# Where VectorE runs the second stream of a modulation unit inside a slot of the seven-product scheme

## What is computed

```python
mod_l = (jax.nn.silu(c) @ w_ada[l] + b_ada[l]).reshape(b_, 1, N_MOD, D_MODEL)
mod_c = (jax.nn.silu(c_ctx) @ w_ada[l] + b_ada[l]).reshape(N_MOD, D_MODEL)
...
def swiglu(h, w_in_ff, w_out_ff):
    gu = h @ w_in_ff
    g, u = gu[..., :D_FF], gu[..., D_FF:]
    return (jax.nn.silu(g) * u) @ w_out_ff
```

## Time and profile before

| | us |
|---|---|
| median of 3 runs (2509.43 to 2518.34) | 2512.81 |
| the profiled execution's own time | 2510.58 |
| its span, first to last instruction | 2508.8 |
| TensorE busy in it | 2441.8 (97%) |
| VectorE busy in it | 1760.4 (70%) |

### The profile page before, as it was taken

The page is one execution under the profiler, slowest core; times in us unless marked ns, Lnnn a source line. Parts: engine busy times, 40 slices in busy tenths (PEclk is TensorE's granted clock), DMA queues, the critical chain, the costliest instruction groups (busy, mean ns, idle before and its releaser), DMA issues.

```text
span 2508.8 us, 33516 instructions
## 1 busy us (share of the span) xinstructions
PE 2441.8 (97%) x12904; PEld 2189.9 (87%) x12904; DVE 1760.4 (70%) x2226; ACT 1068.2 (43%) x1497; POOL 486.2 (19%) x355
## 2 busy tenths in 40 slices
PE   7999999999999999999999999999999999999998
PEld 4999998888987899999888999998888777888787
DVE  5799997676576879888766799786655687522233
ACT  5344433444453743444354544443444555412222
POOL 0344440000500034543000244550000500000000
PEclk9999999999999999999999999999999999999999
DMA  6233336542111243333644433337433203422221
GB/s 256 110 126 131 145 126 252 184 158 83 52 33 66 101 160 134 117 116 128 247 159 148 168 110 126 133 142 256 173 131 108 84 18 135 168 100 97 87 101 67
DMA packets 100364, 328.29 MB, mean 131 GB/s; under 512 B 7809, under 2 KB 38049, under 8 KB 86945
## 3 DMA queue, kind: packets, MB, share of 16 engines
q1 hardware_dynamic: 83040, 316.33, 35.1%
q10 hardware_dynamic: 17218, 10.55, 1.4%
HBM read 318.28 MB, written 8.57 MB: 130 GB/s over the span
## 4 chain that ended last, share of the span: by engine, by line
PE 78%; DVE 13%; issue 5%; DMA 2%; ACT 2%; ACTq 0%; SPq 0%; DVEq 0%
PE ps L2217 29%; PE ps L2177 19%; PE ps L2165 17%; PE ps L931 5%; DVE junk L1772 3%; DVE w_all L2022 2%; DMA acc<-w_ada_t 1%; DVE w_all L1752 1%; PE ps L2259 1%; DVE arena L672 1%; PE ps L1000 1%; PE ps L1071 1%; PE ps L1058 1%; PE ps L955 1%; PE ps L2269 1%
## 5 line engine op out<-in xcount | busy, mean ns | idle before, releaser
L2217 PE MATMUL ps<-w_all,hj_all 128*128 128x512 f32 x2856 | 656.3, 391 | 6.4 <-DVE arena L831 2.5
L2217 PEld LDWEIGHTS ps<-w_all,hj_all 128*128 128x128 f32 x2856 | 535.1, 188 | 119.9 <-issue 3.7
L1752 DVE TENSOR_TENSOR w_all<-raw,w_all 128x2048 fp32r<-128x2048 f32 x156 | 360.5, 2311 | 294.2 <-ACT w_all L1390 294.1
L2177 PE MATMUL ps<-xn_hi,w_all 128*128 128x384 f32 x1728 | 454.1, 336 | 11.7 <-DVE gate_row L2073 11.1
L2165 PE MATMUL ps<-xn_hi,w_all 128*128 128x384 f32 (+2 forms) x1600 | 423.5, 348 | 8.9 <-DVE xn_lo L1830 7.6
L1390 ACT ACTIVATE w_all<-raw 128x2048 fp32r<-128x2048 f32 x157 | 296.9, 1891 | 242.4 <-PE ps L2217 204.6
L1772 DVE SCALAR_TENSOR_TENSOR junk<-acc,silu_row 128x1024 bf16<-128x1024 f32 x224 | 329.8, 1472 | 15.8 <-issue 6.0
L2177 PEld LDWEIGHTS ps<-xn_hi,w_all 128*128 128x128 f32 x1728 | 313.2, 188 | 19.1 <-DVE gate_row L2073 19.0
L2165 PEld LDWEIGHTS ps<-xn_hi,w_all 128*128 128x128 f32 x1600 | 288.8, 189 | 32.3 <-DVE xn_lo L1830 7.8
L2177 PE MATMUL ps<-xn_lo,w_all 128*128 128x384 f32 x864 | 288.7, 334 | 0.0
L2165 PE MATMUL ps<-xn_lo,w_all 128*128 128x384 f32 (+2 forms) x800 | 277.7, 347 | 0.0
(11 more groups left out here) (236 smaller groups left out, 3077.4 us busy)
## 6 DMA issues: line engine op xcount, KB each, us to landing
raw<-w_ff_in SPq DMA_DIRECT2D x104, 1024.0 KB, 4.8
raw<-w_ff_out SPq DMA_DIRECT2D x77, 1024.0 KB, 5.0
acc<-w_ada_t SPq DMA_DIRECT2D x128, 512.0 KB, 3.3
raw<-w_out SPq DMA_DIRECT2D x16, 1024.0 KB, 4.9
raw<-w_in SPq DMA_DIRECT2D x12, 1024.0 KB, 5.7
x<-x_in SPq DMA_DIRECT2D x12, 512.0 KB, 10.8
gate_row<-gate_out_rows ACTq DMA_DIRECT2D x12, 512.0 KB, 7.4
x_out<-x SPq DMA_DIRECT2D x12, 512.0 KB, 9.0
```

Of the source, the lines that this page charges most:

```text
L1752: nc.vector.tensor_tensor(w_lo[par][:, 0:width], raw[par][:, 0:width], w_hi[par][:, 0:width].bitcast(F32), ALU.subtract).then_inc(S["w_lo" ...
L2177: ins = mm(ps[:, bank_, 0:GW], w[:, c], x_[:, k, :], start=start and k == 0 and a == 0, stop=k == 3 and a == 2, skip_group_check=True)
L2217: ins = mm(ps[:, 2 * i + hf, :], xx[:, i * P:(i + 1) * P], w[:, c, hf * 512:(hf + 1) * 512], start=first and c == 0 and a == 0, stop=last ...
```

## The change

The unit is written as two calls of a new function, one for each stream. In a fast slot the first unit's first stream stays where it was, and its second stream now stands behind sum B and low part 1 (in a stage's last slot: behind sum B and the weights of the output product). A slot's second unit, and the units elsewhere, keep both streams together. A unit with one stream has nothing behind sum B. No other engine's instructions change.

```diff
+            def unit_stream(count, half, u, s):
+                n_streams = streams(half)
+                if s >= n_streams:
+                    return
+                if s == 0:
+                    if u == 0:
+                        dve.wait_ge(S["fin_read"], half)
+                    dve.wait_ge(S["ada_raw"], count * 16 + 16)
+                dve.wait_ge(S["ada_used"], count * 2 + (s + START))
+                ins = nc.vector.scalar_tensor_tensor(out=junk[:], in0=acc[:].rearrange("p a n -> p (a n)"), scalar=1.0,
+                                                     in1=silu_row[:, s, :], op0=ALU.mult, op1=ALU.mult,
+                                                     accum_out=ada_col[:, u, s:s + 1])
+                ins.then_inc(S["ada_used"], 2 // n_streams)
+                if u == 3 and s == n_streams - 1:
+                    finish_units(half, half % HALVES, count + 1)
+
             def unit(count, half, u):
...
+                for s in range(2):
+                    unit_stream(count, half, u, s)
...
-                    unit(*units[0])
+                    unit_stream(*units[0], 0)
                     dve.wait_ge(S["snap"], tq * 3 + 3)
                     dve.wait_ge(S["prod"], tq * 6 + 5)
                     nc.vector.tensor_tensor(p5, p5, ps[:, a, 0:GW], ALU.add).then_inc(S["c22"], 1)
...
                     else:
                         split_w(n + 1, par0)
+                    unit_stream(*units[0], 1)
                     dve.wait_ge(S["prod"], tq * 6 + 6)
                     nc.vector.tensor_tensor(u_h, u_h, ps[:, b, 0:GW], ALU.add).then_inc(S["c12"], 1)
```

More of the change, by code:

```diff
@@ L1760, in hj @@
                 nc.vector.tensor_tensor(lo[:, 0:w], hidden(sub, g, c), hi[:, 0:w].bitcast(F32), ALU.subtract).then_inc(S["hj_lo"], 1)
-            def unit(count, half, u):
[L1764 to L1777, removed]
+            def unit_stream(count, half, u, s):
[13 more added lines that the diff above has]
+                    finish_units(half, half % HALVES, count + 1)
+            def unit(count, half, u):
+                for s in range(2):
+                    unit_stream(count, half, u, s)
             def add_bias(h, hl, src):
```

## The result

The changed kernel takes 2520.28 us (median of 14 runs, 2515.19 to 2527.48), the kernel before 2510.39 us (14 runs beside them): a ratio of 1.0038, 95% interval 1.0028 to 1.0047, about 10 us slower. The profiled execution took 2524.53 us, 4.2 above its own median; that of before stood on its median. So the two traces differ by 14.0 us, somewhat more than the kernels do. The length of stage 1 also varies from one execution to the next: two later runs whose program is that of the kernel before up to the last slot of stage 1 have it at 270.2 and 270.9 us, where the trace of before has 272.4. A stage's length can be read to some 2 us there, and to a few tenths in stages 2 and 3.

The account below looks back on a forecast made before the run. The kernel was taken as bound by TensorE, with 17.3 us lost to waits. Terms 11 + 4.6 + 1.0 − 0.6 = 16 on the profiled 2510.6 give 2526.6, about 2528 as median; range 2508 to 2540 us.

Parts of the forecast that it names:

- the gain term: Fast stages: without stream 1 ahead, sum B is ready 2.1 us earlier; at most 17.3 us can be had.
- the loss term: Two-unit slots: the second unit's 3.6 us load is no longer covered; VectorE idles 1.9 us in place of 0.4.
- Stage 1, +11: Stage 1 slot by slot: four groups give 12.4 us, less 1.4 for the earlier sum B at the start.
- two-unit interval: Stage 1, from slot 5's sum B to slot 6's: 15.4 us becomes 16.7, set by VectorE.
- The four groups: Stage 1, groups of four slots (2, 2, 2, 1 units): each 63.0 us where it is 59.9, +3.1.
- The check on stage 1: VectorE's busy time there, less 5 us for GpSimd's hold, plus 27 idle: 277 us, more than the present 272.4.
- End of stage 1, +4.6: Stage 1's last slot: late hidden tile and SyncE's queue behind stream 1 delay the output product by 4.6 us.
- upper bound of 6.0: End of stage 1: the delay if SyncE's queue moves as one piece, 6.0 us; the lower bound was 1.2.
- Stages 2 and 3, +1.0 and −0.6: Stages 2 and 3: 1.2 us back each, 0.2 lost per later two-unit slot, 1.2 at stage 2's end.
- GpSimd's hold, 0.3 us less a slot: VectorE, per slot: stream 1 gains 1.0 us and low part 1 loses 0.7; bounds 0 to 1.0.
- it works as written: Rival: sum B comes early and the 17.3 us come back wholly or in part, about 2500 us; chance 0.10.
- Worse: Rival: low part 1 also waits for late raw weights, 11 slots × 1 to 2 us, 2538 to 2550; chance 0.10.

## Why the prediction was right, and where its sizes were off

- **Direction and mechanism: shown.** VectorE's idle on `DMA acc<-w_ada_t` was to grow "from a few us to some 40, near 1.9 each in stage 1": it grew from 6.0 to 40.0 us, 1.8 each in stage 1. Without the load the loss is gone, and with the load late alone it is there.
- **Time:** 2528 forecast, 2520.28 measured, inside the range; the gain term and the loss term were both there, the net was 9.9 in place of 15. That the sum is this near is in part luck: the terms below were too high by 4.6 and 3.1 us and too low by 2.4, and 3.3 us of the traces' 14.0 belong to none of them.
- **Stage 1, +11: it was +6.4,** the mis-sized term. The two-unit interval was to be 16.7 us; from sum B at 206.16 to the next at 222.51 it is 16.4. The one from slot 4 to slot 5 was to be 16.2 and is 15.7: the second unit's second stream takes 1.2 us there where GpSimd's sums had held it to 2.3, which the prediction left out. The four groups grew by 3.1, 2.4, 1.4 and 1.7 us, 8.6 in all and not 12.4, and the earlier sum B at the stage's start gave 2.3 and not 1.4. The executions vary too: 278.8 or 280.3 us against 270.2, 270.9 or 272.4 is a growth of 6.4 to 10.1, so part of this miss can be chance.
- **The check on stage 1** ("255.5 busy us, less 5 for GpSimd's hold", 277 with the idle) had a wrong busy time: it fell by 14.4, to 241.2. Where sum B waits for TensorE, GpSimd's sum runs out beside that wait and low part 1 is not held at all (1.22 us in slots 4, 8, 12 and 16); and second units are held less.
- **End of stage 1, +4.6: +7.0,** above its upper bound of 6.0. Up to the start of the third output slot it is 5.8, near the 6.0 of a queue that moves as one piece: that slot's weights are issued 3.2 us later against sum B (10.2 us behind it, not 7.0) and take 2.6 us longer to land. What the bound left out is the clock, half for the matmuls behind that wait: 1.2 us more by the fourth slot.
- **Stages 2 and 3, +1.0 and −0.6: +0.2 (−1.1 and 1.3 at its end) and −2.9.** I let each two-unit slot cost 0.2 us in the one behind it. VectorE's slack there took the idle nearly whole: from slot 1 on, stage 3's matmuls wait for sum B once, for 1.0 us.
- **GpSimd's hold, 0.3 us less a slot: 0.36** where sum B does not wait (1.0 off stream 1, 0.6 onto low part 1). Low part 1 takes 1.83 with GpSimd's L1356 beside it, and sum B stays at 0.541 to 0.555 us, as the rule of the Trainium skill (SBUF — State Buffer, Who interferes with whom) has it; the trace agrees.
- **The rival "it works as written" was right for stages 2 and 3,** and would be for stage 1 with an idle under 0.7 us: in the run with stream 1 right behind sum B, where it is 0.5 to 1.3 us, stage 1 lasts 264.4 us and nearly all of it came. Between that and 1.8 us nothing was tried.
- "Worse", low part 1 waiting for raw weights, did not come slot after slot: in the changed kernel's stage 1 low parts wait 3.6 us for ScalarE behind a load, in slot 15 alone. There TensorE then waits 2.2 us for ScalarE, and slot 16's sum B comes 14.7 us after slot 15's where it was 13.5.

## What to carry to other kernels

An instruction that frees a buffer starts a load; moving it later moves the load, and what counts is how much work is left between it and the first reader. Write down that cover (here 3.3 us, then 1.7, against a load of 3.6) before moving anything past it, and look for what else stands in the issuing queue behind that load. When a wait is on one instruction (sum B), move that one forward and let the freeing instruction follow at once: the two orders of stream 1 and low part 1 differ by 16 us.

## What the runs showed of the hardware that I had not expected

At the end of stage 1 the DMA engines are full (1.00 to 1.03 of their time, 396 to 421 GB/s from 398.6 to 410.6 in the changed kernel). A load that goes to the queue 5.9 us later there (against sum B) lets TensorE start the third output slot 5.8 us later, with nothing absorbed. The reloads of `x` stand in the queue ahead of those weights and fill the engines; no run took them away, so that they are the reason is argued, not shown:

```profile
398.60:401.60 3.00, 3.00 (x15) 2.47 (x14) 2.55 (x5) 0.00 (x0) 0.00 (x0) 1.00 1.00 396
401.60:404.60 3.00, 3.00 (x15) 2.49 (x14) 1.83 (x7) 1.60 (x1) 0.00 (x0) 1.00 1.02 414
404.60:407.60 3.00, 0.95 (x5) 0.49 (x4) 2.65 (x2) 1.47 (x4) 0.00 (x0) 1.00 1.03 421
407.60:410.60 3.00, 3.00 (x14) 2.44 (x13) 0.11 (x1) 0.00 (x0) 0.00 (x0) 1.00 1.02 411
```

The granted clock then made the delay longer. Behind the wait of 3.0 us it was 0.50 in the changed kernel, 0.50 behind 2.5 us in the run with the last slot whole, 0.50 behind 4.6 us in the one with the stream behind the tiles, 0.50 behind 4.2 us in the changed kernel without the loads, and 1.00 behind 3.0 us in the one with the change in the last slots alone. In the first two of these the slot behind takes 1.6 us more.
